# Loading the first weight chunk and the input in three pieces each

## What is computed

```python
def _rmsnorm(x, g):
    y = xf * lax.rsqrt(jnp.mean(xf * xf, axis=-1, keepdims=True) + EPS)
    return (y * g.astype(jnp.float32)).astype(x.dtype)

def _ab_mixer(xn, w_in, b_in, ...):
    u = jnp.einsum('bsd,de->bse', xn, w_in) + b_in
    u_conf, u_lru = jnp.split(u, [2 * CONF_WIDTH], axis=-1)
    y_a = _conformer_conv(u_conf, ...)   # val * sigmoid(gate), causal conv of 31 taps, norm, silu
    y_b = _rglru_block(u_lru, ...)       # causal conv of 4 taps, two gates, a linear recurrence
    y = jnp.concatenate([y_a, y_b], axis=-1)
    return jnp.einsum('bse,ed->bsd', y, w_out)
```

## Time and profile before

| | us |
|---|---|
| median of 3 runs | 2041.3 (2041.07 to 2042.13) |
| the profiled execution | 2040.8 |
| its span in the trace | 2039.0 |
| TensorE busy | 1973.0 (97%) |
| TensorE's first matmul starts | 9.47 |
| short convolution starts | 53.98 |
| long convolution starts | 74.32 |
| 16 experts' pairs, layer 0 | from about 954 |

### The profile page before, as it was taken

The page is one execution under the profiler, slowest core; times in us unless marked ns, Lnnn a source line. Parts: engine busy times, 40 slices in busy tenths (PEclk is TensorE's granted clock), DMA queues, the critical chain, the costliest instruction groups (busy, mean ns, idle before and its releaser), DMA issues.

```text
span 2039.0 us, 25122 instructions
## 1 busy us (share of the span) xinstructions
PE 1973.0 (97%) x10310; PEld 1335.8 (66%) x10310; DVE 582.1 (29%) x1351; ACT 424.1 (21%) x961; POOL 12.9 (1%) x34
## 2 busy tenths in 40 slices
PE   8999999999999999998999999999998999999998
PEld 7798888957988888666455445445885455545544
DVE  3277450422555603422111011102233011101111
ACT  2440000322301101322221222122102222122212
POOL 1000000000001000000000000000000000000000
PEclk9998999989999999989999999999999999999999
DMA  9645576432357753213999999999544999999995
GB/s 334 199 170 218 236 305 247 166 111 84 137 233 285 306 220 132 83 42 123 400 429 429 427 429 429 428 429 428 208 148 157 400 430 427 429 428 428 428 429 226
DMA packets 51580, 591.24 MB, mean 290 GB/s; under 512 B 6305, under 2 KB 14761, under 8 KB 15794
## 3 DMA queue, kind: packets, MB, share of 16 engines
q1 hardware_dynamic: 51218, 588.09, 71.0%
q10 hardware_dynamic: 288, 2.10, 0.3%
HBM read 584.69 MB, written 1.05 MB: 287 GB/s over the span
## 4 chain that ended last, share of the span: by engine, by line
PE 70%; DMA 24%; DVE 4%; issue 1%; SPq 0%; ACT 0%; DVEq 0%
PE ps L436 24%; DMA ring<-in_w_up 22%; PE ps L1077 15%; PE ps L668 7%; PE ps L1167 4%; PE ps L1059 2%; PE ps L1065 2%; PE ps L711 2%; PE ps L495 2%; DVE work L1690 1%; DMA ring<-in_w_ada 1%; PE ps L583 1%; PE ps L462 1%; PE ps L511 1%; PE ps L526 1%
## 5 line engine op out<-in xcount | busy, mean ns | idle before, releaser
L1077 PE MATMUL ps<-ring,work 128*64 128x512 f32 x2048 | 450.3, 593 | 12.7 <-DMA ring<-in_w_up 12.2
L436 PE MATMUL ps<-h,ring 128*128 128x256 f32 x2064 | 457.1, 383 | 3.0 <-DVE h L1952 2.2
L436 PEld LDWEIGHTS ps<-h,ring 128*128 128x128 f32 x2064 | 394.0, 192 | 58.8 <-issue 4.0
L1077 PEld LDWEIGHTS ps<-ring,work 128*64 128x64 f32 x2048 | 151.2, 137 | 305.1 <-issue 290.4
L1349 ACT ACTIVATE work<-ps 128x512 f32<-128x512 f32 (+1 forms) x186 | 95.7, 519 | 715.0 <-PE ps L436 302.0
L1167 PE MATMUL ps<-ring,work 128*64 128x512 f32 x1024 | 226.8, 595 | 1.6 <-DVE work L2150 1.6
L1349 ACT ACTIVATE work<-ps,ada,scale_g 128x128 f32<-128x128 f32 x256 | 96.2, 456 | 411.3 <-PE ps L1059 411.3
L2141 DVE TENSOR_TENSOR work<-ps,work 128x512 f32<-128x512 f32 x32 | 22.1, 692 | 551.9 <-ACT work L1349 551.9
L1167 PEld LDWEIGHTS ps<-ring,work 128*64 128x64 f32 x1024 | 70.6, 137 | 133.6 <-issue 128.0
L668 PE MATMUL ps<-work,ring 128*128 128x256 f32 (+1 forms) x704 | 150.0, 376 | 3.9 <-DVE work L1867 3.9
L668 PEld LDWEIGHTS ps<-work,ring 128*128 128x128 f32 x704 | 131.3, 192 | 22.0 <-DVE work L1867 4.6
(11 more groups left out here) (295 smaller groups left out, 1282.2 us busy)
## 6 DMA issues: line engine op xcount, KB each, us to landing
ring<-in_w_gate SPq DMA_DIRECT2D x64, 2048.0 KB, 15.0
ring<-in_w_up SPq DMA_DIRECT2D x64, 2048.0 KB, 17.3
ring<-in_w_down SPq DMA_DIRECT2D x64, 2048.0 KB, 12.2
ring<-in_w_ada SPq DMA_DIRECT2D x24, 2048.0 KB, 8.5
ring<-in_w_ff_gate SPq DMA_DIRECT2D x10, 2048.0 KB, 14.8
ring<-in_w_ff_up SPq DMA_DIRECT2D x10, 2048.0 KB, 12.8
ring<-in_w_ff_down SPq DMA_DIRECT2D x8, 2048.0 KB, 10.9
ring<-in_ml_w_in SPq DMA_DIRECT2D x6, 2048.0 KB, 10.7
```

Source lines behind the costliest of these rows:

```text
L436: last = mm(ps[:, b, 0:T], w[:, k, m * P:(m + 1) * P], rhs[:, k, :], start=(k == 0), stop=(k == nk - 1))
L1077: last = mm(ps[e * CAP:(e + 1) * CAP, j, :], xg[:, k, e * CAP:(e + 1) * CAP], w[e][:, k, :], start=(k == 0), stop=(k == KT - 1))
```

## The change

`START = (0, 2, 4)` cuts the row groups into pieces of 2, 2 and 4. Chunk 0 is loaded in these three pieces by SyncE and `x` by ScalarE. The first 16 columns of `vec` (the two layers' `pre_mix_g`) are loaded ahead of everything, the other 436 behind chunk 0. Semaphore `start_loaded` becomes three, one for each piece: 48 for the first (gains, weights, x), 32 for the second (weights, x), 16 for the third (x; its weights count on `slot_loaded[0]`). A new `vec_loaded` covers the rest of `vec`. TensorE, ScalarE and VectorE wait piece by piece. To make room for the new semaphores three pairs of others are merged, with the same order of counts (`lru_decay` and `lru_root`, `f_abs` and `gate_m`, `z_sq` and `z_root`), and the expert part's first four gate steps carry their stop flag on k = 3.

```diff
+START = (0, 2, 4)
+START_DMAS = (48, 32, 16)
...
-        start_loaded = sem("start_loaded")
+        start_loaded = [sem(f"start_loaded_{i}") for i in range(3)]
+        vec_loaded = sem("vec_loaded")
...
-                    if n == 0 and k == KT // 2:
-                        pe.wait_ge(slot_loaded[0], 16)
+                    if n == 0 and k in START:
+                        pe.wait_ge(start_loaded[START.index(k)], START_DMAS[START.index(k)])
+                        if k == START[-1]:
+                            pe.wait_ge(slot_loaded[0], 16)
...
-            pe.wait_ge(start_loaded, 16 * 3)
...
-            def gate_step(k, w, j=0):
+            def gate_step(k, w, j=0, last_k=KT - 1):
...
-                              start=(k == 0), stop=(k == KT - 1))
+                              start=(k == 0), stop=(k == last_k), skip_group_check=True)
...
-            sp.dma_start(vec[:], a["vec"]).then_inc(start_loaded, 16)
-            half = SLOT // 2
-            sp.dma_start(ring[:, 0, 0:half].rearrange("p (k c) -> p k c", k=KT // 2),
-                         chunks[0][0][:, 0:KT // 2, :]).then_inc(start_loaded, 16)
-            sp.dma_start(ring[:, 0, half:SLOT].rearrange("p (k c) -> p k c", k=KT // 2),
-                         chunks[0][0][:, KT // 2:KT, :]).then_inc(slot_loaded[0], 16)
+            sp.dma_start(vec[:, 0:16], a["vec"][:, 0:16]).then_inc(start_loaded[0], 16)
+            for i, (k, end) in enumerate(zip(START, START[1:] + (KT,))):
+                sp.dma_start(ring[:, 0, k * CH:end * CH].rearrange("p (k c) -> p k c", c=CH),
+                             chunks[0][0][:, k:end, :]).then_inc(start_loaded[i] if end < KT else slot_loaded[0], 16)
+            sp.dma_start(vec[:, 16:NVEC], a["vec"][:, 16:NVEC]).then_inc(vec_loaded, 16)
...
-            act.dma_start(x[:], a["x"]).then_inc(start_loaded, 16)
+            for i, (k, end) in enumerate(zip(START, START[1:] + (KT,))):
+                act.dma_start(x[:, k:end, :], a["x"][:, k:end, :]).then_inc(start_loaded[i], 16)
             act.wait_ge(memsets, 8 + HEADS)
-            act.wait_ge(start_loaded, 16 * 3)
-            squares(x, done=S["sq_sum"])
+            for k in range(KT):
+                if k in START:
+                    act.wait_ge(start_loaded[START.index(k)], START_DMAS[START.index(k)])
+                turn.give(A(sq[:, k, :], x[:, k, :], ACT.Square), S["sq_sum"])
+            act.wait_ge(vec_loaded, 16)
...
             dve.wait_ge(memsets, 8 + HEADS)
-            dve.wait_ge(start_loaded, 16 * 3)
             for k in range(KT):
+                if k in START:
+                    dve.wait_ge(start_loaded[START.index(k)], START_DMAS[START.index(k)])
                 turn.give(V.tensor_scalar(u[:, k, :], x[:, k, :], gain("pre_mix_g", 0)[:, k:k + 1], None, ALU.mult),
                           S["u_ready"])
+            dve.wait_ge(vec_loaded, 16)
```

More of the change, by code:

```diff
@@ L301, in build @@
         names = ("start_act ada_raw squares roots x_ready x_added h_ready u_ready scaled sq_sum summed pool_step glu_gate glu "
[L302 removed]
+                 "rec_in gelu_in lru_conv ada_made lru_gate lam_ready h_scaled x_squares lru_powers lru_mixed lru_taps_made tiles_convolved ln_mean "
                  "ln_centred ln_normed ln_sigmoid mixed proj_copied ffn_sig ffn_gate_read hidden mq mo mv "
[L304 to L305 removed]
+                 "gates_tok gates_head gate_args f_ln gate_a row_max gate_expm acol_ready exponents decays weighted "
+                 "den_read head_out sums_read y_ready f_sum f_root f_ready att_copied u_gelu z_gelu z_centred z_stats z_normed "
                  "k_rope_read q_rope_read rotated maxima exps turned_dve turned_act sink_ready sink_exp norms_ready norm_rows att_normed logits_read "
@@ L1040, in experts @@
                 for k in range(KT // 2):
-                    gate_step(k, [matrices(first, e)[2][0] for e in range(2)])
+                    last = gate_step(k, [matrices(first, e)[2][0] for e in range(2)], last_k=KT // 2 - 1)
                 for b in (0, 1):
@@ L1432, in _ @@
             for j in range(HTL):
-                turn.give(A(rate[:, j, :], th[:, j, :], ACT.Exp, scale=lamt[:, 24 + j:25 + j]), S["lru_decay"])
-            turn.own(S["lru_decay"])
+                turn.give(A(rate[:, j, :], th[:, j, :], ACT.Exp, scale=lamt[:, 24 + j:25 + j]), S["lru_powers"])
+            turn.own(S["lru_powers"])
             for j in range(HTL):
@@ L1437, in _ @@
             turn.own(achain)
[L1438 removed]
+            turn.give(A(den_a, th, ACT.Sqrt), S["lru_powers"])
             turn.own(S["gelu_in"])
[L1440 removed]
+            turn.give(A(gin[:], gin[:], ACT.Gelu_apprx_tanh), S["lru_powers"])
             for j in range(HTL):
@@ L1511, in _ @@
             value_out(0, 0)
-            turn.take(S["f_abs"])
+            turn.take(S["gate_args"])
             turn.give(A(ghead[:, 2, :], ghead[:, 2, :], ACT.Exp, scale=-1.0), achain)
@@ L1517, in _ @@
             value_out(1, 0)
-            turn.take(S["gate_m"])
+            turn.take(S["gate_args"])
             turn.give(A(ghead[:, 3, :], ghead[:, 3, :], ACT.Exp, scale=-1.0), S["gate_expm"])
@@ L1566, in _ @@
                     for t in range(TT):
-                        turn.give(A(z_a[:, t, :], zc[:, t, :], ACT.Square, accum_out=small[:, 4 + t:5 + t]), S["z_sq"])
-                    turn.own(S["z_sq"])
-                    turn.give(A(small[:, 6:8], small[:, 4:6], ACT.Sqrt, bias=eps[:], scale=1.0 / HALF), S["z_root"])
+                        turn.give(A(z_a[:, t, :], zc[:, t, :], ACT.Square, accum_out=small[:, 4 + t:5 + t]), S["z_stats"])
+                    turn.own(S["z_stats"])
+                    turn.give(A(small[:, 6:8], small[:, 4:6], ACT.Sqrt, bias=eps[:], scale=1.0 / HALF), S["z_stats"])
                 if i % 2 == 0:
@@ L1795, in _ @@
             step(V.tensor_tensor(bx[:], bx[:], xr[:], ALU.mult))
-            turn.take(S["lru_decay"], HTL)
-            turn.take(S["lru_root"])
+            turn.take(S["lru_powers"], HTL)
+            turn.take(S["lru_powers"])
             step(stt(den_a, rate, 1.0, den_a, ALU.add, ALU.mult))
@@ L1891, in _ @@
             step(V.tensor_copy(ghead[:, 0:2, :], tile()[0:8].rearrange("p (a b) -> p a b", a=2)), S["gates_head"])
-            step(stt(ghead[:, 2, :], ghead[:, 1, :], -1.0, ghead[:, 1, :], ALU.mult, ALU.max), S["f_abs"])
+            step(stt(ghead[:, 2, :], ghead[:, 1, :], -1.0, ghead[:, 1, :], ALU.mult, ALU.max), S["gate_args"])
             turn.take(S["f_ln"])
@@ L1898, in _ @@
                  S["row_max"])
-            step(V.tensor_tensor(ghead[:, 3, :], ghead[:, 3, :], ghead[:, 2, :], ALU.add), S["gate_m"])
+            step(V.tensor_tensor(ghead[:, 3, :], ghead[:, 3, :], ghead[:, 2, :], ALU.add), S["gate_args"])
             step(V.tensor_copy(acol[:], tile()[:, 0:16].rearrange("p (a b) -> p a b", a=TT)), S["acol_ready"])
@@ L2000, in _ @@
                 if i == 3:
-                    turn.take(S["z_root"])
-                    turn.take(S["z_sq"], TT)
+                    turn.take(S["z_stats"])
+                    turn.take(S["z_stats"], TT)
                     step(V.reciprocal(small[:, 8:10], small[:, 6:8]))
```

5 lines of the change are left out of this document (removed).

## The result

| | before | after |
|---|---|---|
| median of 12 runs each, us | 2041.2 (2039.5 to 2046.6) | 2047.5 (2044.2 to 2050.7) |
| ratio | | 1.003, 95% interval 1.0021 to 1.004 |
| profiled execution, span | 2040.8, 2039.0 | 2046.53, 2044.7 |
| first matmul | 9.47 | 8.71 |
| first 48 records of chunk 0 end | 22.47 | 21.54 |

A forecast was written before the change was run, and what follows sets the result against it. It took the full DMA line, which sets when the spreads' copies land, as the bound: 2040.8 us profiled, - 0.3 (second spread's end) + 0.1 (added DMAs) = 2040.6, that execution 0.5 under the median, so 2041.1 us; range 2039.0 to 2042.9.

The forecast's parts named there:

- TensorE comes to the short convolution at 51.2 us: Start 2.8 us earlier carried to the short convolution, where TensorE waits 0.7 us for copies landing at 51.8 us.
- Rival A: Second spread's landing follows its issue, so the gain of 2.8 us goes through: 2038.5 us; chance 0.14.
- I take 0.1 us in all: Cost of four added DMAs in the load stream: 0.1 us taken, at most 1.6 us.
- Below nothing I see no reason: Lower bound for the cost of four added DMAs in the stream: not under 0 us.
- rival B: Every added DMA holds up the stream: at most 1.6 us (2042.9 us), far end 2048.5 us; chance 0.02.
- the landing of the first piece: First loads at the kernel's head land at 6.1 us (5.3 to 6.8), so TensorE starts at 6.7 us.
- holds up on ScalarE the norm's root: The wait for vec_loaded at ScalarE's root in the head: wanted at 20 us or later, data there at 16.2 us.
- waits some 3 us instead of 1.01: TensorE, arriving at 71.2 us, idles before the long convolution for the second spread; the remaining 2.1 us gained are gone.
- behind 74 us all goes on at the old distances: After the long convolution's start, all later stages keep their old spacing, with no further gain or loss.
- C: Second piece late in chunk 0, so TensorE stops and resumes at slow pace: 4.8 us later, 2046.1 us; chance 0.02.
- D: First piece at the head lands no earlier, as DMAs share engines: all stays at 2041.3 us; chance 0.03.

The follow-up runs named there:

- e9: The changed kernel with every piece (of x, chunk 0 and vec) stored as an array of its own in memory; 2043.38 us, ratio 1.0009.
- e11: The changed kernel with 12 and 22 idle matmul records ahead of TensorE's waits for the two spreads; 2045.11 us, ratio 1.0019.
- e1: The kernel before with only x cut in three DMAs and the first half of chunk 0 in two, engines waiting for all; 2047.95 us, ratio 1.0027.
- e5: The kernel of e1 with every piece an array of its own in memory; 2036.88 us, ratio 0.9984 against before.
- e3: The changed kernel with ScalarE's wait for vec_loaded moved behind the norm's root; 2046.26 us, ratio 1.0023 against before.
- e7: The kernel before with both spreads issued one weight chunk earlier in SyncE's queue; 2034.82 us, ratio 0.9974.
- e6: The kernel before with only x cut into three DMAs, all engines still waiting for all of it; 2038.49 us, ratio 0.9997.
- e13: The kernel before with SyncE and ScalarE starting their first DMA some 2.1 us later; 2042.08 us, ratio 1.0007.
- e12: The kernel before with only the first half of chunk 0 cut into two DMAs; 2041.23 us, ratio 1.0005.
- e2: The kernel before with only vec split, 16 columns first and 436 behind chunk 0; 2040.59 us, ratio 0.9996.

## Why the prediction was wrong

**Right: what bounds the start.** "TensorE comes to the short convolution at 51.2 us" and waits there, and at the long one the lead is gone: e9 shows it with 51.89 and 74.85 us, and e11 once more that an earlier issue doesn't give an earlier landing. Rival A, the gain that goes through, appears in no kernel as long as the order of the queue stands.

**Wrong: "I take 0.1 us in all" for the pieces in the stream**, with 1.6 us as the upper bound. This is the step that failed. In the changed kernel the last copies land 5.2 and 9.6 us late; with the cuts of `x` and of the first half alone (e1) it is 4.2 and 6.0, and with the same pieces from arrays of their own (e5) 0.7 and 1.6. The price was looked for in the number of DMAs (0 to 0.39 us each, from copies between SBUF and SBUF), and the length of rows was set aside because 423 GB/s were seen in the window in which "`vec`, with rows of 1.8 KB, landed". But these rows adjoin in memory: `vec` is loaded whole. They say nothing of 2 KB cut out of 8 KB. Among the first loads of before only the halves of chunk 0 are cut out of longer rows, 8 KB out of 16 KB, and the stream moved 423 GB/s with them; of shorter ones no row tells, so the bound should have been open upwards. "Below nothing I see no reason" was thought about, above 1.6 us hardly (rival B, 0.02). How the slow head becomes late copies stays open.

**Wrong by the same step: the landing of the first piece.** Its bytes were moved along the rates of the earlier trace rows, which the change itself lowers. It landed at 8.10 us instead of 6.1 (5.3 to 6.8), and TensorE started at 8.71, outside 5.9 to 7.4. One reading in it is a little off: the 0.46 MB up to `vec` and as much of `x` had moved by 3.4 us, so that landing trails by 2.0 us, not 1.8; this moves the late end by 0.2 us. With adjoining rows it landed at 5.38 and TensorE started at 6.00 us: the method was sound, its rate was not.

**Wrong: `vec_loaded` "holds up on ScalarE the norm's root", wanted only later.** True of the wait itself, not of the table load ahead of the root, which took over the wait for TensorE's sums: 1.28 us in the row at 22.06 us. e3 gives it back (chunk 1 1.5 us earlier). The order of ScalarE's instructions shows this without a run.

**Not priced: half clock behind a stop.** TensorE "waits some 3 us instead of 1.01" stands there as if waiting cost only itself. In the changed kernel the two stops add 1.4 us and 2.1 us in the convolutions (and 0.3 in L555), in e9 a stop of 3.56 us adds 2.9, so that in its trace the cut without slow reads ends the long convolution 3.4 us later than before. Not every such stop does it (e5: 3.16 us and nothing added).

**Wrong: "behind 74 us all goes on at the old distances".** The span made up 6.1 of 11.8 us. Without it the kernel would have been some 12 us slower; that the forecast missed by 6 us and not by 12 is luck of those intervals.

**Rivals.** B had the right sign, and its far end of 2048.5 us is near the measured 2047.5, but by luck. Its rule, a price for every added DMA, would be 2.4 us each here, but e5 and e9 have the same DMAs as e1 and the changed kernel, and their second spread lands only 1.6 and 0.6 us late. C and D did not come: no stop inside chunk 0, and a first piece that was a little earlier.

## What to carry to other kernels

Before a load is cut into pieces, look at how the pieces lie in memory: with rows of 2 KB cut out of 8 KB the first loads ran at half to two thirds of the rate, and the cure that worked is to store each piece as its own array. An earlier start is worth nothing while a later stage waits for something in a full DMA line; shorten or reorder the line first (e7 takes the stop away, for 0.7 us), and then ask for the start. A total that moves by 0.3% can come from another part of the kernel: look at landmarks of the stage that was changed before calling it a gain. A stop that grows from 1 to 3 us is not neutral, as TensorE may run at half clock behind it, and a second wait given to an instruction behind a table load can put the load in sequence.

## What the runs showed of the hardware

- Reads with 2 KB rows 8 KB apart: 192 to 197 GB/s in 2 to 4 us against 290 to 304 for the same loads with adjoining rows (e6 and e1 against before and e5), at a DMA share of 0.81 to 0.84 against 0.88 to 0.91. The share does not tell such a loss; the GB/s beside it do.
- Where `x` and the weights are both cut (e1), the stream is 0.67 MB behind by 8 us and 1.45 by 59.5, and the copies land 4.2 and 6.0 us late. With only `x` cut (e6) 0.42 MB behind become 0.05, and with a head that is merely 2.1 us late (e13) 0.91 become 0.82. Why is open.
- The long convolution behind its stop: 13.95 us behind none, 14.02 behind 1.01, 1.80, 2.98 (e11, filled) and 3.16 us (e5); 15.46 behind 3.06 (e12), 15.71 behind 3.08 (e3); 16.91 behind 3.56 (e9) and 3.58 (e2); 15.35 to 16.72 behind 3.65 to 3.81; 16.16 behind 5.74. Nearly the same stop is sometimes followed by half clock and sometimes not (e5 and e3). With idle matmuls in the stop the convolutions kept their old lengths (e11, one trace).
- Later intervals at half clock come and go between kernels that differ only in their first 100 us, and move the total by some 6 us (after, e5 and e7 against before). The same kernel spreads too: 35 executions of before, taken beside e9, lie between 2035.6 and 2047.8 us.
